# Filter and modulation stage: the second layer of the filter net ahead of all modulation items, eight items instead of four ahead of the filter products

## The reference

```python
    hid = jnp.sin(lp["hy_freq"][0].astype(F32) * (feat @ lp["hy_w1"].astype(F32) + lp["hy_b1"].astype(F32)))
    hid = jnp.sin(lp["hy_freq"][1].astype(F32) * (hid @ lp["hy_w2"].astype(F32) + lp["hy_b2"].astype(F32)))
    filt = (hid @ lp["hy_w3"].astype(F32)) * jnp.exp(-t01 * deltas)
    filt = filt.reshape(n, HY_ORDER, 2, HY_D)
    fwd, bwd = filt[:, :, 0], filt[:, :, 1]
    k2 = jnp.concatenate([fwd, jnp.zeros((1, HY_ORDER, HY_D), F32), jnp.flip(bwd[1:], axis=0)], axis=0)
    return k2 / jnp.sum(jnp.abs(k2), axis=0, keepdims=True)
```

## Time and profile before

| | us |
|---|---|
| median of 3 runs | 2758.31 |
| profiled execution | 2756.62 |
| span of the profiled execution | 2754.8 |
| TensorE busy in the span | 2490.2 (90%) |
| VectorE busy | 1634.3 (59%) |
| ScalarE busy | 943.5 (34%) |
| GpSimd busy | 289.5 (11%) |

### The profile page before, as it was taken

One profiled execution on the slowest core, in us unless ns is written; L12 is line 12 of the kernel. 1 busy time (PEld: TensorE's weight loads), 2 busy tenths in 40 slices (PEclk: granted clock), 3 DMA queues, 4 the chain that ended last, 5 costly groups with the idle time before them and its releaser, 6 DMA issues. The chain is left out here.

```text
span 2754.8 us, 30553 instructions
## 1 busy us (share of the span) xinstructions
PE 2490.2 (90%) x11832; PEld 1994.5 (72%) x11832; DVE 1634.3 (59%) x1639; ACT 943.5 (34%) x1086; POOL 289.5 (11%) x242
## 2 busy tenths in 40 slices
PE   7879967699996989999999999999859999999994
PEld 3338856578884878878778787787748888888871
DVE  5443368623323564343397532757678888888875
ACT  4132310133321433300111200003137778777763
POOL 3210000000003210000000000100001222122210
PEclk9989989899998889999999999999869999999997
DMA  5341135212325122211111111544459999999956
GB/s 170 130 138 39 46 123 174 86 39 87 115 79 185 54 59 65 65 43 44 46 46 46 39 43 50 173 140 168 183 212 363 371 361 359 367 366 383 390 196 244
DMA packets 91342, 433.30 MB, mean 157 GB/s; under 512 B 15864, under 2 KB 25352, under 8 KB 76522
## 3 DMA queue, kind: packets, MB, share of 16 engines
q1 hardware_dynamic: 65194, 355.71, 35.1%
q0 software_dynamic: 26048, 76.20, 7.9%
HBM read 399.41 MB, written 53.41 MB: 164 GB/s over the span
## 5 line engine op out<-in xcount | busy, mean ns | idle before, releaser
L360 PE MATMUL ps<-uT_upper_rest,ring_rest 128*128 128x512 f32 x1360 | 541.3, 398 | 0.0
L360 PEld LDWEIGHTS ps<-uT_upper_rest,ring_rest 128*128 128x128 f32 x1360 | 258.9, 190 | 66.1
L2526 PE MATMUL ps<-ex_u_raw_rest,uT_rest 128*128 128x256 f32 x560 | 156.8, 280 | 0.0
L360 PE MATMUL ps<-uT_upper_rest,xbc_upper 128*128 128x512 f32 x336 | 136.5, 406 | 7.6 <-DVE ring_rest L782 7.6
L360 PE MATMUL ps<-uT_upper_rest,cs_upper 128*128 128x512 f32 x320 | 130.0, 406 | 11.2 <-DVE ring_rest L782 6.0
L2524 PE MATMUL ps<-ring_rest,uT_rest 128*128 128x256 f32 (+1 forms) x416 | 134.7, 324 | 3.1 <-DVE uT_rest L2833 2.4
L360 PE MATMUL ps<-uT_rest,xbc_upper 128*128 128x512 f32 x336 | 134.9, 402 | 0.0
L2524 PE MATMUL ps<-ex_upper,uT_rest 128*128 128x256 f32 (+1 forms) x424 | 134.8, 318 | 0.0
L2525 PE MATMUL ps<-ex_upper,uT_rest 128*128 128x256 f32 (+1 forms) x424 | 134.0, 316 | 0.0
L2525 PE MATMUL ps<-ring_rest,uT_rest 128*128 128x256 f32 (+1 forms) x416 | 132.7, 319 | 0.0
L360 PE MATMUL ps<-uT_rest,cs_upper 128*128 128x512 f32 x320 | 128.6, 402 | 0.0
(11 more groups left out here) (474 smaller groups left out, 6130.9 us busy)
## 6 DMA issues: line engine op xcount, KB each, us to landing
sb_spare<-in_ex_g SPq DMA_DIRECT2D x35, 2048.0 KB
ex_u_raw<-in_ex_u SPq DMA_DIRECT2D x35, 2048.0 KB, 10.0
sb_merged<-in_ex_d SPq DMA_DIRECT2D x35, 2048.0 KB
ring<-in_conv SPq DMA_DIRECT2D x32, 512.0 KB, 3.3
ring<-in_w_gate SPq DMA_DIRECT2D x32, 512.0 KB, 3.3
md_piece<-in_w_late POOLq DMA_DIRECT2D x32, 512.0 KB, 5.2
ring<-in_w_ssd SPq DMA_DIRECT2D x21, 512.0 KB, 3.2
ring<-in_w_mod SPq DMA_DIRECT2D x16, 512.0 KB, 3.4
```

The lines of the kernel that those rows point to most:

```text
L360: last = self.nc.tensor.matmul(out, weight, x[:, k, lo:hi], start=(k == 0 and n == 0), stop=(k == kt - 1 and n == 2))
L2526: return nc.tensor.matmul(out, left_up, w_lo, start=False, stop=last)
```

## The change

A constant `AHEAD = 8` gives how many modulation items stand ahead of the filter steps (before: 4, written into the code). Layer 2 of the net, and with it the wait for the first sine, moves ahead of the wait for the SiLU and of all items. ScalarE's copies follow: four ahead of the loop instead of two, and the later ones two pairs further on. The number of instructions of every kind stays as it was. Since one line is added at the top of the function and two fall away, line numbers in the changed kernel are shifted by one.

```diff
+    AHEAD = 8
@@ TensorE
                 mm.then_inc(pre_ready, 1)
-                pe.wait_ge(silu_c, 1)
-                modulation(0)
-                modulation(1)
                 pe.wait_ge(hid_ready, 1)
                 for h in range(2):
                     part = slice(h * HY_HID, (h + 1) * HY_HID)
                     mm = nc.tensor.matmul(ps[part, 1, :], w2[part, :], hid[part, 0, :], start=True, stop=True)
                 mm.then_inc(pre_ready, 1)
-                modulation(2)
-                modulation(3)
+                pe.wait_ge(silu_c, 1)
+                for m in range(AHEAD):
+                    modulation(m)
                 pe.wait_ge(hid_ready, 2)
                 pe.wait_ge(w3_in, 16)
                 for n in range(len(halves)):
                     filters(n)
-                    if n + 4 < EARLY:
-                        modulation(n + 4)
+                    if n + AHEAD < EARLY:
+                        modulation(n + AHEAD)
@@ ScalarE
                 decay(0)
                 decay(1)
-                modulated(0)
-                modulated(1)
+                for pair in range(AHEAD // 2):
+                    modulated(pair)
...
-                    if n % 2 and n // 2 + 2 < EARLY // 2:
-                        modulated(n // 2 + 2)
+                    if n % 2 and (n + AHEAD) // 2 < EARLY // 2:
+                        modulated((n + AHEAD) // 2)
```

## The result

| | before | changed |
|---|---|---|
| median of 20 runs each, us | 2757.37 | 2762.47 |
| lowest and highest | 2752.69, 2762.17 | 2757.86, 2782.03 |
| ratio, 95% interval | | 1.0028 (1.0014 to 1.0041) |
| profiled execution, us | 2756.62 | 2759.65 |
| its span | 2754.8 | 2757.9 |

The change makes the kernel slower, by 5.1 us between the medians. The profiled executions are only 3.0 us apart, and the changed kernel's runs lie much wider.

What follows compares the result with a forecast made beforehand. TensorE was taken to bound the stage's middle, VectorE and GpSimd its end. Layer 2 earlier, step 1 1.39 us later and slower item-free steps (1.2 us) gave +2.6 us: 2758.31 + 2.6 = 2760.9 us, range 2755.5 to 2766.0.

Steps and rivals of the forecast that it cites:

- the range: Whole kernel: median between 2755.5 and 2766.0 us, the forecast's bounds plus scatter, leaving both far rivals out.
- the 0.2% to which I gave 0.80: Whole kernel: change within about 0.2% (5.5 us), counted as same, chance 0.80; slower 0.14, faster 0.06.
- the 3.5 us of scatter: Whole kernel: about 3.5 us for the scatter of a median, included in the predicted 2755.5 to 2766.0 us.
- the sum: Stage end: 96.38 us instead of 93.79, +2.6 us, with bounds +1.7 to +4.3.
- Layer 2 first: Stage start: layer 2 begins at 11.86, lasts 1.97 us; second sine at 18.29 instead of 24.51, 6.2 us earlier.
- Item 4 and step 0: Stage start on TensorE: item 4 at 24.52, step 0 at 31.88 instead of 25.19; step 1 loses 1.39 us.
- full clock behind a wait of 1.6 us: TensorE at item 4: items at 1.84 us after the wait; one item at half clock would add 1.7 us.
- Steps without items at 4.06 us: Stage's last eight filter steps: pairs of 8.11 us, 32.48 us in all, a second loss of 1.2 us.
- The rival in which the steps run free: Last eight filter steps: no stretched pairs, GpSimd at 2.59 us each, stage end 87.1, 6.7 us less; chance 0.06.
- The one thing it can hand on is the moment at which its last engine is done: Stage's closing barrier: only the stage's end time was taken to affect what follows; the +2.6 us passed on whole.
- one more sign of being wrong: Stages after the changed one: the prediction is wrong if they change by more than the stage does.

Runs made afterwards that it cites:

- e4: The changed kernel run again without modification, among the runs of another series: 2765.97 us (12 runs), ratio 1.0024 to before.
- e6: The changed kernel with eight extra filter-like products (64 rows, result unused) on TensorE behind the stage's transposes: 2767.09 us (7 runs).
- e7: The changed kernel with GpSimd's additions of the last eight filter steps cut to 32 of 512 channels: 2768.84 us (4 runs), not comparable, other work later.
- e10: The changed kernel with seven extra products of all 128 rows (result unused) on TensorE at the stage's end: 2761.08 us (11 runs), ratio 1.0016 to before.
- e3: Before with two extra VectorE operations at the stage's end, a pause of 2.49 us: 2765.88 us (5 runs), ratio 1.0033.
- e9: Before with twelve extra products of all 128 rows (result unused) on TensorE at the stage's end: 2756.52 us (11 runs), ratio 0.9999.
- e5: Before with ten extra filter-like products (64 rows, result unused) on TensorE behind the stage's transposes: 2767.01 us (6 runs).
- e2: Before with eight items ahead of the filter steps, layer 2 still behind item 1: 2768.21 us (5 runs), ratio 1.0041.
- e12: The changed kernel with six items ahead of the filter steps instead of eight, layer 2 still first: 2761.06 us in its one run.
- e1: The changed kernel with four items ahead instead of eight, so layer 2 first is the only part kept: 2753.48 us (12 runs), ratio 0.9983 to before.
- e8: The changed kernel with two items ahead instead of eight, layer 2 still first: 2754.83 us (12 runs), ratio 0.9997 to before.
- e11: Layer 2 first and four items ahead, plus twelve extra products of all 128 rows at the stage's end: 2749.57 us (8 runs), ratio 0.9971 to before.

## Why the prediction was right or wrong

The measured 2762.47 us lies inside the range, slower was the side that was forecast, and in the profiled execution the stage ends within 0.3 us of the forecast. In size the forecast was half of what came (2.6 against 5.1 us), and the ratio, 1.0028, is past the 0.2% to which I gave 0.80. That the time still fell into the range is owed to the 3.5 us of scatter in it, not to a term of the sum; in that measure it was luck, and the later median of the same kernel (e4, 8.3 us above before) lies at the range's upper end.

- *Layer 2 first.* Right: 11.87 (11.86 forecast), 1.97 us as taken from layer 1, second sine at 18.30 (18.29).
- *Item 4 and step 0.* Right in the profile: 24.53 (24.52), 31.61 (31.88). The clock is where the sum was too small. I took full clock behind a wait of 1.6 us. The wait was 2.25 us, since items 0 to 3 took 8.50 us, less than the 9.06 of before. Two of the five profiles of the changed kind (its own, e4, e6, e7, e10) met the half clock: after waits of 2.82 and 2.76 us the four items took 8.81 us, after 2.25, 2.14 and 1.61 us 7.15.
- *Before is not fixed either.* In before the first item lands at 13.64, in its variants e3 and e9 at 12.80 and 12.81, and the stage ends at 93.27 and 93.11; e5 ends it at 92.39. The changed stage doesn't profit from an early landing, because its items wait for layer 2 until 13.8. Over four profiles each (before, e3 without its pause, e5, e9; the changed kernel, e4, e6, e10) the stage ends at 93.1 and at 97.0 on average: 3.9 us, not 2.6. The earlier landing is a term that I missed in the sum, 0.7 us on average; the rest of the difference comes from the half clock at item 4 (1.7 us in two of the four).
- *Steps without items at 4.06 us.* Right: the end stretch took 96.12 - 63.62 = 32.50 us (32.48 forecast), and e7 shows the cause. The rival in which the steps run free did not come about.
- *"The one thing it can hand on is the moment at which its last engine is done".* This step failed. The stage also hands on TensorE's clock. In before, e2, the changed kernel, e6 and e7 the opening took 29.8 to 30.0 us, in e12 29.4; in e1, e3, e4, e5 and e8 36.9 to 37.3; with the clock held up, 28.0. The 6.9 us are larger than the whole sum of 2.6, and a profiled execution's time follows from stage end and opening: what comes after the opening takes 2627.0 to 2632.3 us in eleven of the profiled executions (all but e7, with its other work, e12 with 2636.3 and e11 with 2638.7). This does not sort the runs of one kernel, of which only the profiled one is seen: the profile of e3, with the long opening, is the shortest of its five.
- *The sum over all.* With full-array products ahead of the barrier the difference is 4.6 us (e10 against e9), which the stage nearly covers (3.9 by the four profiles each, 4.8 in these two). Without them the first 20 runs have 5.1 and the runs of e4 8.3. That the rest is how often an execution meets the long opening fits these numbers, but is argued, not shown. Half clock at item 4 and the long opening would together lift the changed kernel's profiled 2759.65 to 2768.2; five of its first 20 executions lie above that, three of them at 2776.95 to 2782.03, and no profile caught one of these.

I had named one more sign of being wrong, later stages that change by more than the stage does. By the profiles of before and of the changed kernel they don't (0.8 us against 2.3). By the medians it came: 5.1 us less the stage's 2.3 leaves 2.8, and in e4 8.3 less 3.9 leaves 4.4.

What stays open: why, as it seems, the changed kernel meets the long opening more often than before. Only one unmodified execution of before is profiled, and it had the short one. The profiles show that with a grant of 1.00 at the barrier the opening took 28.0 us (e9 to e11), and that without such products it began at half clock in all eleven others, after idleness or after products with 64 rows, and took 29.4 to 37.3. Why one moment of starting gets the clock back after 4 us and another after 18 was not settled. Openings were short after 10.91 and 10.92 us of idleness (e2, the changed kernel) and long after the same 10.91 us (e4), so the length of the wait doesn't decide it.

## What to carry to other kernels

Putting fillers ahead of the work that is on the path delays that path. Here four modulation items moved ahead cost 10.2 us in the stage (the changed kernel against e1) and 10.5 (e2 against before), more than their own 4 x 1.84 = 7.4, because step 0 then also stands behind the wait ahead of item 4 and four more steps run without an item between. The good half of the change (layer 2 first) was worth 7.9 us in the stage by itself. Interleaved items also kept VectorE and GpSimd apart: look for operations that stretch beside an addition on GpSimd before making two engines run back to back. And where a stage ends with TensorE waiting, price the next stage's first products at both clocks. Products of the full array in that wait narrowed the scatter here; in before they gained nothing in the median (2756.52 against 2756.75 us), while the version with layer 2 first and four items ahead was 7.2 us under before with them and 4.2 without.

## What the hardware showed unexpectedly

- Ten products that use 64 rows did not hold the clock up: 11 us without a gap at a grant of 0.50 (e5), against 1.00 for twelve products with 128 rows at the same place (e9). The two also differ in operands and in how the products are spread.
- A 2.49 us pause on VectorE at a stage's end made the kernel's median 8.3 us longer (e3).
- Matrix products with one column each (L620, 16 in a group) between the 512-column ones kept TensorE busy at half clock for 14 us in e1 without the grant coming back; it came back at about 105.7 us, within the products with `sb_odd`.
- A collision between VectorE and GpSimd can keep itself going: in e8 VectorE, late in the first steps, took 4.06 us a step on average from step 3 on.
